# Hybrid decoder step on one Trainium2 core: query norms in compact rows, chunks 3 and 5 of the input projection by seven half-sized products

## The chip, the cores and the metric

The kernel runs on one core of a Trainium2 chip. The metric is the device time of one execution in microseconds (us), start to end, for the prompt (256 tokens) and the sample group (8 tokens) together.

## The reference

One layer of a hybrid decoder over 264 tokens, width 1024. All data are float32.

```python
h = rmsnorm(x, attn_norm_w)
proj = jnp.einsum('btd,de->bte', h, w_in)          # 1024 -> 6400
xin, bg, cg, q, k, v, g_conv, g_attn = jnp.split(proj, ...)
conv_out, conv_state = causal_short_conv(cg * xin, conv_prefix, conv_w)   # width 3
y_conv = bg * conv_out
q = rmsnorm(q.reshape(b, T, N_HEADS, HEAD_DIM), q_norm_w)   # per head, 16 heads of 64
k = rmsnorm(k.reshape(b, T, N_KV, HEAD_DIM), k_norm_w)
y_attn = window attention (window 128, relative bias, sinks)
merged = sigmoid(g_conv) * y_conv + sigmoid(g_attn) * y_attn
x = x + merged @ w_out
x = x + moe_ffn(rmsnorm(x))      # top 4 of 32 experts, clamped SwiGLU
```

Outputs are y for both groups and the new convolution, key and value states.

## The kernel before

**Order of the work.** The kernel first projects the normed tokens, held transposed (features on partitions, 264 tokens as columns), then runs attention and convolution in between, then the output projection and routing, then streams the weights of all 32 experts (two at a time, `pair`). The weights of `w_in` come in 13 chunks of 2 MB (`w_in_chunk`): chunk 0 holds k and v; chunks 1 and 2 q; 3 cg; 4 xin; 5 bg; 6 gc; 7 cg; 8 xin; 9 bg; 10 gc; 11 and 12 ga. cg, xin, bg and gc appear twice, for the two halves of the features. An ordinary chunk is four tiles of 128 features, numbered through by `tile_list` (tiles 2 to 5 are chunk 1, 10 to 13 chunk 3, 14 to 17 chunk 4, 18 to 21 chunk 5), each eight products of 128x128 by 264 columns into one of two banks of `pB`. A query tile holds two heads' halves and takes sixteen 128x64 products that run in pairs.

**Chunks by seven products.** The chunks named in `SEVEN` (line 81: 6, 7, 9 to 12) are computed as a 2x2 block product with seven block products instead of eight (the Strassen-Winograd scheme). One product (`product`, line 2020, slots s = 0 to 6) is eight matmuls of 132 columns. It needs four sums of weight blocks (`add_weights`, L1409, on VectorE, into a ring slot of their own), sums of token blocks shared by all chunks (`side1` to `side4`, L1422), and VectorE reads the results out of PSUM (`seven`, L1345). Products 0 to 3 use the banks of `pB`, 4 to 6 the upper half of `pA`, where attention scores of two key blocks also lie.

**The order is written out by hand** in `plan` (line 196) and the tables above it. `STEPS` is one list of steps, walked by each engine in turn; a step is placed "after" a tile or a slot, and `slot(c, s)` is product s of chunk c. `SUM_STEPS` places the weight sums, `SIDE_STEPS` the token sums, `UNIT_STEPS` the seven steps of each attention unit (scores, bias, peak, exp, norm, turn, values). `FILLS_OF` counts how many fills of the two banks of `pM` (`misc_bank`) each step makes.

**Query norms.** Every query tile is squared on ScalarE (L1074). For two tiles at a time TensorE adds the 64 squares of each head by four 64x64 matmuls of ones ("squares"), so that each sum stands on all 64 rows of its head. VectorE scales them (L1508, L1512), ScalarE takes the root (L1077), VectorE the reciprocal of the whole 128x264 tile (L1518) and the product with the queries (L1520).

**Convolution.** On an xin tile VectorE multiplies it with cg (L1473), then does the three taps: three operations on the 256 prompt columns (L1482, L1485) and three on the 8 sample columns, with the convolution state as input for two of them (L1483, L1487). On tile 0 of them it waits for the stores of keys and values, whose staging rows in `yc` the result overwrites.

**Ring and queues.** The ring has six slots of 2 MB. `RING` lists weights and sums in order; each entry takes the next slot and waits until TensorE has left the chunk six entries earlier. SyncE (SP) issues all weight loads in order, and between them some of the 32x32 block moves of the attention probabilities (`move_blocks`; the rest are on GpSimd's queue). Loads of expert weights start when TensorE starts chunk 12.

## Time and profile before

| what | us |
|---|---|
| median of 3 runs | 1150.89 (1149.01 to 1151.21) |
| profiled execution | 1149.04 |
| its span, first to last instruction | 1147.1 |
| TensorE busy | 1094.3 (95%) |
| VectorE busy | 445.6 (39%) |
| ScalarE busy | 184.8 (16%) |
| GpSimd busy | 88.7 (8%) |

The chain that ended last is 61% TensorE and 37% DMA. Busy shares are averages over stages: the projection, up to about 200 us, and the experts' stream behind it have different limits, so the stages are to be read apart.

### The profile page before, as it was taken

How to read it: one execution, taken by the hardware profiler on the slowest of the kernel's cores; microseconds unless marked ns; L12 is line 12 of the kernel's file. 1: busy time of each engine (PE TensorE's matmuls, PEld its weight loads, DVE VectorE, ACT ScalarE, POOL GpSimd, SP SyncE). 2: the span in 40 equal slices, each digit the busy share in tenths (PEclk: the TensorE clock that was granted, in tenths of full speed). 3: DMA queues.
4: the chain of work that ended last, by engine and by line, in shares of the span. 5: the costliest groups of instructions: out<-in, count | busy, mean ns of one | idle time of the engine just before them, and what ended most of it. 6: DMA issues, size and time to landing. Idle time of an engine off the chain costs nothing.

```text
span 1147.1 us, 14808 instructions
## 1 busy us (share of the span) xinstructions
PE 1094.3 (95%) x5914; PEld 494.8 (43%) x5943; DVE 445.6 (39%) x882; ACT 184.8 (16%) x394; POOL 88.7 (8%) x161
## 2 busy tenths in 40 slices
PE   9999999999999999999899999999999999999997
PEld 6688899553333333333333333333333333333332
DVE  4867786753343233233223232323232323232322
ACT  2133231211321101010101010101010101010101
POOL 1775115000000000000000000000000000000000
PEclk9999999999999999999999999999999999999999
DMA  9945639999999999999999999999999999999996
GB/s 320 329 135 158 196 92 350 414 359 419 397 419 428 416 432 431 431 431 434 430 431 432 434 431 433 430 431 434 430 433 432 433 432 428 433 434 430 425 424 284
DMA packets 53204, 444.35 MB, mean 387 GB/s; under 512 B 13100, under 2 KB 19372, under 8 KB 35740
## 3 DMA queue, kind: packets, MB, share of 16 engines
q1 hardware_dynamic: 46712, 435.83, 91.3%
q0 software_dynamic: 5600, 7.32, 2.4%
q10 hardware_dynamic: 852, 0.64, 0.2%
q8 instruction: 28, 0.46, 0.2%
q14 instruction: 12, 0.10, 0.0%
HBM read 439.78 MB, written 2.37 MB: 385 GB/s over the span
## 4 chain that ended last, share of the span: by engine, by line
PE 61%; DMA 37%; issue 1%; DVE 1%; ACT 0%; SPq 0%; DVEq 0%
PE pA L2001 31%; PE pB L2001 22%; DMA ring<-in_w_up 21%; DMA ring<-in_w_down 10%; PE pM L2001 6%; DMA area<-in_w_up 5%; PE pM L2004 1%; DMA ring<-in_w_in 1%; PE pA L2004 1%; ACT area L1223 0%; DVE x L1848 0%; SPq L775 0%; DVE conv_row L1762 0%; DVE area L1923 0%; DVE x L1928 0%
## 5 line engine op out<-in xcount | busy, mean ns | idle before, releaser
L2001 PE MATMUL pA<-ring,hn 128*64 128x512 f32 x1536 | 352.6, 602 | 23.2 <-DMA ring<-in_w_up 23.2
L2001 PEld LDWEIGHTS pA<-ring,hn 128*64 128x64 f32 x1536 | 105.3, 137 | 219.1 <-issue 185.5
L2001 PE MATMUL pB<-ring,area 128*64 128x512 f32 (+2 forms) x784 | 171.5, 591 | 6.6 <-DMA ring<-in_w_down 5.8
L2001 PE MATMUL pB<-area,ring 128*128 128x132 f32 (+2 forms) x928 | 140.3, 342 | 0.6 <-DMA ring<-in_w_in 0.6
L2001 PE MATMUL pA<-area,hn 128*64 128x512 f32 x512 | 119.3, 610 | 10.4 <-DMA area<-in_w_up 10.4
L2001 PEld LDWEIGHTS pB<-area,ring 128*128 128x128 f32 (+1 forms) x928 | 115.7, 175 | 22.4 <-issue 3.3
L2001 PEld LDWEIGHTS pB<-ring,area 128*64 128x64 f32 (+2 forms) x784 | 58.5, 136 | 101.2 <-issue 87.8
L1848 DVE TENSOR_TENSOR x<-pM,x 128x512 f32<-128x512 f32 x60 | 40.1, 692 | 147.7 <-PE pM L2001 147.7
L1211 ACT ACTIVATE area<-area 128x512 f32<-128x512 f32 x30 | 18.9, 631 | 385.5 <-DVE area L1831 385.5
L1762 DVE COPY conv_row<-pM 128x512 f32<-128x512 f32 x30 | 20.6, 686 | 146.2 <-PE pM L2001 146.2
L2001 PEld LDWEIGHTS pA<-area,hn 128*64 128x64 f32 x512 | 36.1, 139 | 74.6 <-issue 59.7
L2001 PE MATMUL pB<-area 128*64 128x512 f32 (+2 forms) x300 | 66.8, 549 | 1.2 <-DVE area L1292 1.2
L1831 DVE TENSOR_SCALAR area<-pA 128x512 f32<-128x512 f32 x30 | 20.7, 692 | 92.6 <-PE pA L2001 92.6
L1765 DVE TENSOR_TENSOR hn<-pM,fnorm 128x512 f32<-128x512 f32 x30 | 20.7, 692 | 84.9 <-PE pM L2004 84.5
L2001 PE MATMUL pM<-area 128*32 128x256 bf16 (+2 forms) x353 | 49.0, 327 | 2.7 <-issue 2.4
L1873 DVE COPY area<-pB 64x512 f32<-64x512 f32 x15 | 10.4, 694 | 100.0 <-PE pB L2001 100.0
L2001 PEld LDWEIGHTS pM<-area 128*128 128x128 bf16 (+2 forms) x368 | 18.7, 96 | 51.2 <-issue 35.6
L2001 PEld LDWEIGHTS pB<-area 128*64 128x64 f32 (+2 forms) x300 | 20.8, 131 | 35.5 <-issue 31.0
L2001 PE MATMUL pM<-hn,x 128*128 128x512 bf16 x98 | 30.4, 381 | 2.1 <-issue 2.1
L1409 DVE TENSOR_TENSOR ring<-ring 128x1024 f32<-128x1024 f32 x24 | 29.0, 1217 | 0.1
L1223 ACT ACTIVATE area<-pA 128x512 f32<-128x512 f32 x15 | 9.0, 597 | 120.7 <-PE pA L2004 120.7
L2004 PEld LDWEIGHTS pA<-cst,area 128*128 128x128 f32 x120 | 16.8, 210 | 24.3 <-issue 24.3
(351 smaller groups left out, 942.5 us busy)
## 6 DMA issues: line engine op xcount, KB each, us to landing
ring<-in_w_up SPq DMA_DIRECT2D x36, 4096.0 KB, 29.8
ring<-in_w_down SPq DMA_DIRECT2D x18, 4096.0 KB, 29.0
area<-in_w_up SPq DMA_DIRECT2D x12, 4096.0 KB, 30.2
ring<-in_w_up SPq DMA_DIRECT2D x16, 2048.0 KB, 12.8
area<-in_w_down SPq DMA_DIRECT2D x6, 4096.0 KB, 30.0
ring<-in_w_in SPq DMA_DIRECT2D x22, 1024.0 KB, 12.2
ring<-in_w_down SPq DMA_DIRECT2D x16, 1024.0 KB, 10.6
ring<-in_w_up SPq DMA_DIRECT2D x16, 1024.0 KB, 8.4
```

The lines of the kernel that those rows point to most:

```text
L1211: nc.scalar.activation(early_sig if kind == "first" else sig[:, e, :], early_glu if kind == "first" else glu[:, e, :], ACT.Sigmoid, scale= ...
L1223: nc.scalar.activation(turned, pA[:, 1024:1536], ACT.Copy).then_inc(aT_ready, 1)
L1409: V.tensor_tensor(out, x0, x1, op).then_inc(sums_ready, 1)
L1762: return V.tensor_copy(xrow[:, 512 * half:512 * half + 512], b)
L1765: return V.tensor_tensor(xsT[:, 4 * half:4 * half + 4, :], b.rearrange("p (k s) -> p k s", k=4), fw[:, 4 * half:4 * half + 4, :], ALU.mult)
L1831: V.tensor_scalar(gl, u[:, 0, e], LIMIT, None, ALU.min).then_inc(glu_ready, 1)
L1848: V.tensor_tensor(xo, bank(k), xo, ALU.add).then_inc(misc_free, 1)
L1873: V.tensor_copy(y_pair[64:128, 512:1024], pB[64:128, 1, :]).then_inc(y_ready_dve, 1)
L2001: return pe.matmul(out, w, m, start=start, stop=stop, skip_group_check=True)
L2004: return pe.transpose(out, src, ident[0:src.shape[0], 0:src.shape[0]])
```

## The change

**Query norms.** The eight query tiles form two groups of four. "q_sum" adds the squares of four tiles (eight heads) by four matmuls whose weights are a 128x32 cut of the two-block matrix: 16 columns for one head and 16 for the other. The sums of four tiles lie in four bands of 32 rows, so one scaling, one root (ScalarE) and one reciprocal ("q_inverse") serve eight heads. "q_norm" spreads one row per head back over 64 rows, by four matmuls of 32 rows by 64 columns whose weights are one column of the identity, repeated. VectorE multiplies the queries straight from PSUM. There are two q_sum and four q_norm steps where there were four steps "squares".

**Chunks 3 and 5** join `SEVEN`. Since the queries and the old places of the token sums are in use that early, the sums for these two chunks stand in `yc` and `cx` (`early1`, `early2`, `early4`) and ScalarE copies them to the old places later ("side_move").

**Taps.** The first tap of each tile goes to ScalarE ("first_tap", with the wait for the stores of keys and values), the other two come later on VectorE ("taps") and take the sample columns along. The taps on the convolution state are done for four tiles at once ("state_taps").

**Steps** of attention units 0 and 1 and the sample attention are placed anew. With eight chunks in `SEVEN` the ring's entries shift: weights 5 wait for chunk 0, weights 6 for chunk 2, weights 7 for chunk 3, weights 8 for chunk 5 (before: none, 0, 2 and 4). From weights 9 on each waits for the same chunk as before. The diff, cut:

```diff
-SEVEN = (6, 7, 9, 10, 11, 12)
+SEVEN = (3, 5, 6, 7, 9, 10, 11, 12)
+EARLY_SIDES = (3, 5)
...
-UNIT_STEPS = [(11, 12, 12, 13, 13, 18, 19),
-              (18, 18, 19, 19, 20, slot(6, 5), slot(7, 3)),
+UNIT_STEPS = [(slot(3, 2), slot(3, 4), slot(3, 4), slot(3, 6), slot(3, 6), slot(5, 1), slot(5, 3)),
+              (slot(5, 0), slot(5, 1), slot(5, 2), slot(5, 3), slot(5, 5), slot(6, 5), slot(7, 3)),
...
-SIDE_STEPS = [20, 21, slot(6, 2), slot(6, 3), slot(9, 0)]
-SUM_STEPS = {6: (19, 20, slot(6, 0), slot(6, 1)),
+SIDE_STEPS = [5, 6, 7, 8, slot(9, 0)]
+STATE_TAP_STEPS = [6, slot(7, 4)]
+FIRST_TAP_STEPS = [15, 16, 16, 17, 30, 31, 32, 33]
+TAP_STEPS = [16, 17, slot(5, 0), slot(5, 1), 31, 32, 33, slot(9, 0)]
+SIDE_MOVES = [slot(5, 2), slot(5, 4), slot(6, 0)]
+SUM_STEPS = {3: (7, 8, 9, slot(3, 0)),
+             5: (slot(3, 1), slot(3, 2), slot(3, 6), 14),
+             6: (slot(5, 3), slot(5, 5), slot(6, 0), slot(6, 1)),
...
+    for g, at in enumerate(((6, 7, 8, 9), (slot(3, 1), slot(3, 3), slot(3, 5), slot(3, 6)))):
+        for n, what in enumerate((("q_sum", g), ("q_inverse", g), ("q_norm", (g, 0)), ("q_norm", (g, 1)))):
+            after[at[n]].append(what)
...
-    for n, what in ((13, "s_scores"), (14, "s_exp"), (16, "s_norm"), (18, "s_turn"), (20, "s_values")):
+    for n, what in ((14, "s_scores"), (15, "s_exp"), (16, "s_norm"), (slot(5, 1), "s_turn"), (slot(5, 4), "s_values")):
...
+                elif what == "first_tap":
...
+                    nc.scalar.activation(yc[:, a, 0:SEQ], cx[:, a, 0:SEQ], ACT.Copy,
+                                         scale=cols[:, V_CONV + a:V_CONV + a + 1]).then_inc(tap_ready, 1)
...
+                elif what == "q_inverse":
+                    dve.wait_ge(rt_out, a + 2)
+                    V.reciprocal(q_rows[a], q_rows[a]).then_inc(q_inverted, 1)
+                elif what == "q_norm":
+                    g, n = a
+                    for i in range(2):
+                        dst = qT[:, 4 * g + 2 * n + i, :]
+                        V.scalar_tensor_tensor(out=dst, in0=dst, scalar=cols[:, V_QN:V_QN + 1], in1=misc_bank()[:, 0:NT],
+                                               op0=ALU.mult, op1=ALU.mult).then_inc(misc_free, 1)
...
+                elif what == "taps":
...
+                    link(V.scalar_tensor_tensor(out=yc[:, a, 0:SEQ], in0=cx[:, a, 1:1 + SEQ], scalar=w[1],
+                                                in1=yc[:, a, 0:SEQ], op0=ALU.mult, op1=ALU.add))
+                    link(V.scalar_tensor_tensor(out=yc[:, a, :], in0=cx[:, a, 2:], scalar=w[2],
+                                                in1=yc[:, a, :], op0=ALU.mult, op1=ALU.add))
...
+                elif what == "q_sum":
+                    b = misc_bank()
+                    pe.wait_ge(sq_ready, 5 + 4 * a)
+                    for n in range(4):
+                        mm = matmul(b[32 * n:32 * n + 32, 0:NT], cst[:, C_BLK + 48:C_BLK + 80], squares[4 * a + n + 1])
+                    mm.then_inc(misc_full, 1)
+                elif what == "q_norm":
+                    g, n = a
                     b = [misc_bank(), misc_bank()]
+                    pe.wait_ge(q_inverted, g + 1)
+                    for i in range(2):
+                        r = slice(32 * (2 * n + i), 32 * (2 * n + i) + 32)
+                        for h in range(2):
+                            row_of = ident[r, r.start + 16 * h:r.start + 16 * h + 1].to_broadcast([32, HD])
+                            mm = matmul(b[i][HD * h:HD * h + HD, 0:NT], row_of, q_rows[g][r])
+                        mm.then_inc(misc_full, 1)
```

**What the tables move.** TensorE, from chunk 2's last tiles to the end of chunk 3, before (four full tiles; the matmuls into pM from tmp and rt are "squares", those into pA the scores of unit 0):

```order
L2001 MATMUL pB<-area,ring 64x264 x16
L2001 MATMUL pB<-area,ring 128x264 x8
L2001 MATMUL pM<-tmp,cst 64x264
L2001 MATMUL pM<-rt,cst 64x264
L2001 MATMUL pM<-tmp,cst 64x264
L2001 MATMUL pM<-rt,cst 64x264
L2001 MATMUL pB<-area,ring 128x264 x8
L2001 MATMUL pA<-keys,area 128x128 x8
L2001 MATMUL pB<-area,ring 128x264 x16
```

The same place now; pM 32x264 is q_sum, pM 64x264 q_norm:

```order
L2049 MATMUL pM<-area,cst 64x264 x4
L2049 MATMUL pB<-area,ring 128x132 x16
L2049 MATMUL pM<-area,cst 32x264 x4
L2049 MATMUL pB<-area,ring 128x132 x8
L2049 MATMUL pA<-keys,area 128x128 x8
L2049 MATMUL pB<-area,ring 128x132 x8
L2049 MATMUL pA<-area,ring 128x132 x16
L2049 MATMUL pM<-area,cst 64x264 x4
L2049 MATMUL pA<-area,ring 128x132 x8
L2049 MATMUL pM<-area,cst 64x264 x4
```

Four tiles became seven products, with four norm steps on and between them instead of one behind the first tile.

VectorE between slots 3 and 6 of chunk 3 now (L1390 reads products, L1548 is the reciprocal of eight heads, L1607 to L1622 bias and peak of unit 0, L1553 the queries' multiplication); before, the reciprocals stood behind the single tiles and none behind a product:

```order
L1390 TENSOR_TENSOR rt<-tmp,pB 128x264
L1548 RECIPROCAL area<-area 128x264
L1390 TENSOR_TENSOR area<-rt,pA 128x2x132
L1607 SCALAR_TENSOR_TENSOR area<-pA,area 128x4x128 x2
L1615 TENSOR_REDUCE stat<-area 128x8
L1620 TENSOR_TENSOR stat<-stat,sink 128x8
L1621 TENSOR_SCALAR stat<-stat 128x8
L1622 TENSOR_TENSOR stat<-stat,sink 128x8
L1390 TENSOR_TENSOR area<-rt,pA 128x2x132
L1553 SCALAR_TENSOR_TENSOR area<-area,cols,pM 128x264 x2
L1390 TENSOR_TENSOR area<-tmp,pA 128x2x132
```

What moved: the multiplication of q_norm (1,0), the L1553 row here, stands behind bias and peak of unit 0.

VectorE around bias and peak of unit 1, before (L1491 are the bg tiles, L1617 the turned sample probabilities, L1584 the block transpose of unit 0):

```order
L1491 TENSOR_TENSOR area<-pB,area 128x264
L1617 COPY hn<-pM 128x512
L1584 STREAM_TRANSPOSE area<-hn 128x1024
L1559 SCALAR_TENSOR_TENSOR area<-pA,area 128x640 x2
L1491 TENSOR_TENSOR area<-pB,area 128x264
L1409 TENSOR_TENSOR ring<-ring 128x1024
L1567 TENSOR_REDUCE stat<-area 128x8
L1572 TENSOR_TENSOR stat<-stat,sink 128x8
L1573 TENSOR_SCALAR stat<-stat 128x8
L1574 TENSOR_TENSOR stat<-stat,sink 128x8
```

And now (the first row reads slot (5,1), L1574 and L1576 are the taps of tile 3, L1415 multiplies the result of slot (5,2)):

```order
L1390 TENSOR_TENSOR tmp<-tmp,pB 128x264
L1665 COPY hn<-pM 128x512
L1574 SCALAR_TENSOR_TENSOR area<-area,cols 128x256
L1576 SCALAR_TENSOR_TENSOR area<-area,cols 128x264
L1632 STREAM_TRANSPOSE area<-hn 128x1024
L1607 SCALAR_TENSOR_TENSOR area<-pA,area 128x640 x2
L1415 TENSOR_TENSOR area<-pB,area 128x2x132
L1615 TENSOR_REDUCE stat<-area 128x8
L1620 TENSOR_TENSOR stat<-stat,sink 128x8
L1621 TENSOR_SCALAR stat<-stat 128x8
L1622 TENSOR_TENSOR stat<-stat,sink 128x8
```

A weight sum has left the piece and two taps have come in; the piece now lies between slots of chunk 5 instead of full tiles.

## Rows read from the trace of the kernel before

**Rows 1.** Busy us by stage: span, engines, PEclk, DMA share, GB/s.
```profile
0.00:173.00 173.00, 171.14 (x1354) 138.97 (x1355) 127.31 (x263) 52.48 (x171) 72.82 (x130) 1.00 0.66 204
173.00:240.00 67.00, 66.70 (x430) 47.50 (x429) 44.53 (x122) 13.70 (x33) 15.84 (x32) 1.00 0.98 382
...
500.00:1147.00 647.00, 599.23 (x2884) 215.21 (x2901) 183.49 (x313) 75.45 (x124) 0.00 (x0) 0.99 0.99 425
```

**Rows 2.** What TensorE waited for, 0 to 240 us: total, times, longest.
```profile
PE pB L2001 <- DVE area L1292: 1.2, 1, 1.2
PE pB L2001 <- DMA ring<-in_w_in: 0.6, 1, 0.6
PE pM L2001 <- DVE mask L1752: 0.3, 1, 0.3
```

**Rows 3.** The chain of waits, in order of time: start us, us, what.
```profile
29.95 0.60 PE pM L2001 x8
30.56 7.27 PE pB L2001 x64
...
46.31 7.47 PE pB L2001 x48
...
54.39 3.76 PE pB L2001 x16
...
67.15 18.00 PE pB L2001 x80
85.15 0.44 PE pM L2004 x4
...
90.59 1.01 PE pM L2001 x8
...
96.39 10.96 PE pB L2001 x80
...
171.68 7.20 PE pB L2001 x64
```

**Rows 4.** Timeline of VectorE, 34 to 92 us: start us, us, line, operation.
```profile
34.28 0.49 DVE L1520 SCALAR_TENSOR_TENSOR area<-area,cols,tmp 128x264 f32<-128x264 f32 x1
...
61.39 1.28 DVE L1559 SCALAR_TENSOR_TENSOR area<-pA,area 128x512 f32<-128x512 f32 x2
...
64.37 0.17 DVE L1574 TENSOR_TENSOR stat<-stat,sink 128x8 f32<-128x8 f32 x1
...
85.25 0.43 DVE L1491 TENSOR_TENSOR area<-pB,area 128x264 f32<-128x264 f32 x1 [1.35 <-PE pB L2001]
85.62 0.69 DVE L1617 COPY hn<-pM 128x512 f32<-128x512 f32 x1
86.23 1.24 DVE L1584 STREAM_TRANSPOSE area<-hn 128x1024 f32<-128x1024 f32 x1
87.39 1.52 DVE L1559 SCALAR_TENSOR_TENSOR area<-pA,area 128x640 f32<-128x640 f32 x2
...
92.18 1.48 DVE L1567 TENSOR_REDUCE stat<-area 128x8 f32<-128x1280 f32 x1
```

**Rows 5.** Groups of VectorE, 0 to 200 us: count, busy us, mean ns, idle.
```profile
L1409 DVE TENSOR_TENSOR ring<-ring 128x1024 f32<-128x1024 f32 x24 | 29.0, 1217 | 0.1
L1518 DVE RECIPROCAL tmp<-tmp 128x264 f32<-128x264 f32 x6 | 10.8, 1799 | 2.0 <-ACT tmp L1077 2.0
L1485 DVE SCALAR_TENSOR_TENSOR area<-area,cols 128x256 f32<-128x256 f32 x16 | 7.8, 485 | 0.6
```

**Rows 6.** Timeline of ScalarE, first exponential of unit 1.
```profile
94.30 0.43 ACT L1121 ACTIVATE area<-area,stat 128x160 f32<-128x160 f32 x1 [18.17 <-DVE stat L1574]
```

**Rows 7.** Timeline of SyncE's DMA issues: start us, us of issuing, what.
```profile
82.06 0.92 SPq L762 DMA_DIRECT2D ring<-in_w_in  x2
102.20 3.41 SPq L747 DMA_DIRECT2D hn<-area  x5
...
185.74 0.34 SPq L840 DMA_DIRECT2D ring<-in_w_up  x1
```

More of the change, by code:

```diff
@@ L202, in plan @@
     after[0].append(("square_in", 0))
[L203 to L210 removed]
+    after[2] += [("square", 0), ("qknorm", 0), ("bias_table", 0)]
+    for g, at in enumerate(((6, 7, 8, 9), (slot(3, 1), slot(3, 3), slot(3, 5), slot(3, 6)))):
+        for n, what in enumerate((("q_sum", g), ("q_inverse", g), ("q_norm", (g, 0)), ("q_norm", (g, 1)))):
+            after[at[n]].append(what)
+    for j in range(1, 9):
+        after[j + 1].append(("square_in", j))
     after[3].append(("v_rows", 0))
@@ L218, in plan @@
         after[step].append(("sides", n))
+    for n, step in enumerate(SIDE_MOVES):
+        after[step].append(("side_move", n))
+    for t in range(KT):
+        after[FIRST_TAP_STEPS[t]].append(("first_tap", t))
+        after[TAP_STEPS[t]].append(("taps", t))
+    for n, step in enumerate(STATE_TAP_STEPS):
+        after[step].append(("state_taps", n))
     for c in SEVEN:
@@ L261 @@
           ("gather", 1), ("count", 1), ("gather", 2)]
-FILLS_OF = {"slot": 0, "sides": 0, "sums": 0, "half": 0, "tile": 0, "square_in": 0, "split": 0, "qknorm": 0, "scores": 0, "bias": 0, "exp": 0, "norm": 0, "turn": 0, "peak": 0, "s_norm": 0, "s_exp": 0, "out": 0, "rms": 0,
+FILLS_OF = {"slot": 0, "sides": 0, "sums": 0, "half": 0, "tile": 0, "square_in": 0, "side_move": 0, "q_inverse": 0, "first_tap": 0, "taps": 0, "state_taps": 0, "split": 0, "qknorm": 0, "scores": 0, "bias": 0, "exp": 0, "norm": 0, "turn": 0, "peak": 0, "s_norm": 0, "s_exp": 0, "out": 0, "rms": 0,
             "v_rows": 0, "k_rows": 0, "state_cols": 0, "cache_cols": 0, "conv_rows": 0,
-            "s_split": 0, "part": 0, "ahead": 0, "gather": 0, "s_scores": 2, "squares": 2}
+            "s_split": 0, "part": 0, "ahead": 0, "gather": 0, "s_scores": 2, "q_norm": 2}
 FILL, _n = {}, 0
@@ L414, in build @@
         rstd = tmp[:, 1, :]
-        squares = [tmp[:, 0, :], tmp[:, 1, :], rt[:]]
+        squares = [tmp[:, 0, :]] + 2 * [ya[:, 4 + n, :] for n in range(4)]
+        q_rows = [cx[:, 6 + g, 2:] for g in range(2)]
         table = [one.take(8 * w).rearrange("p (h s) -> p h s", h=8) for w in WIDTH]
@@ L670, in build, with in_pairs @@
         side4 = hn[:, 1, 256:256 + K2 * HALF].rearrange("p (k n) -> p k n", k=K2)
+        early1 = yc[:, 4:6, :].rearrange("p k n -> p (k n)").rearrange("p (k n) -> p k n", k=K2)
+        early2 = yc[:, 6:8, :].rearrange("p k n -> p (k n)").rearrange("p (k n) -> p k n", k=K2)
+        early4 = cx[:, 4:6, 2:].rearrange("p a (b n) -> p a b n", b=2)
+        def in_pairs(side):
+            return side.rearrange("p (a b) n -> p a b n", b=2)
         side3 = [one.take(KT * NT // 4).rearrange("p (k n) -> p k n", k=K2), b12]
@@ new lines, in _ @@
+                elif what == "qknorm":
+                    dve.wait_ge(rt_out, 1)
+                    link(V.reciprocal(squares[0], squares[0]))
+                    link(V.scalar_tensor_tensor(out=kT, in0=kT, scalar=cols[:, V_KN:V_KN + 1], in1=squares[0],
+                                                op0=ALU.mult, op1=ALU.mult))
+                    V.tensor_copy(kR[:], kT[:, 0:SEQ][:, ::-1]).then_inc(qk_normed, 1)
+                elif what == "q_sum":
+                    V.tensor_scalar(q_rows[a], misc_bank()[:, 0:NT], 1.0 / HD, EPS, ALU.mult, ALU.add).then_inc(misc_free, 1)
+                elif what == "q_inverse":
[7 more added lines that the diff above has]
+                                               op0=ALU.mult, op1=ALU.mult).then_inc(misc_free, 1)
+                    if a == (1, 1):
+                        dve.wait_ge(misc_free, FILL["q_norm", (1, 1)])
@@ L2063, in product @@
                     for k in range(K2):
-                        mm = matmul(b[:, HALF * n:HALF * n + HALF], w[:, k, 128 * n:128 * n + 128], m[:, k, :],
+                        mm = matmul(b[:, HALF * n:HALF * n + HALF], w[:, k, 128 * n:128 * n + 128],
+                                    m[:, k // 2, k % 2] if s == 6 and early else m[:, k, :],
                                     start=(first and n == k == 0), stop=(k == K2 - 1))
```

127 lines of the change are left out of this document (59 added, 68 removed).

## The prediction

> **What bounds the kernel now.** I read the busy time by stage first [rows 1]. Up to 173 us TensorE is busy for 171.1 of 173 us while the DMA engines are at 0.66 of their time. From 173 us on the DMA share is 0.98 and 0.99. The granted clock is 1.00 up to 240 us, the upper of its two levels (2.4 GHz), and 0.99 in the last stage, so the clock plays no part. The waits of TensorE come next [rows 2]: up to 240 us it waits for anything in three places, 2.1 us in all, and none of them lies in the projection. In order of time its work is an unbroken row of products [rows 3]. So the projection is bound by TensorE with VectorE just behind it. The loads of the expert weights, which set the second half, are issued as TensorE frees the ring (the first at 185.74 us [rows 7], at the start of chunk 12). A microsecond won or lost on TensorE before that moves the whole stream by a microsecond. That is the measure for each part.
>
> **The path's own work.** An ordinary tile costs 18.00 / 5 = 3.60 us and a chunk of four 14.40; a product of the scheme costs 7.20 / 4 = 1.80 us and a chunk of seven 12.60 [rows 3]. Two chunks: **-3.60 us**.
> Query norms: before, four steps of 0.60 us each (one stands at 29.95 [rows 3]). Now six: two that sum four heads' squares into 32 rows each, four that spread them back. None of these shapes is in the trace. A step can't be shorter than one pass of its 264 columns, and a query tile does eight such passes in 7.27 / 2 = 3.64 us, so 0.45; if its four matmuls ran one after another it would be 4 x 0.45 = 1.8. The nearest row is the old step, also four matmuls on parts of the array, at 0.60, and I take that: 6 x 0.60 - 4 x 0.60 = **+1.2 us** (bounds +0.3 and +8.4).
> Interruptions: the pair of tiles that starts after a norm step at 46.31 takes 7.47 instead of 7.24 (3.64 + 3.60), and the tile at 54.39 takes 3.76 instead of 3.60 [rows 3]; query tiles after a norm step show nothing (7.27 at 30.56). Three more places now return to full-width products: **+0.45 us**. The Trainium skill's page TensorEngine Tiling (Array Packing), under Key Properties, says that changing the tiling mode drains TensorE. By that rule every one of the six steps would pay on both sides, where the query tiles above pay nothing; its consequence is weighed as rival C.
> Sum of TensorE's work alone: -3.6 + 1.2 + 0.45 = **-1.95 us**. Everything else is whether VectorE keeps up.
>
> **VectorE's work.** It loses eight single reciprocals for two (six fewer, 1.80 us each [rows 5], 10.8 us), loses the first convolution tap of eight tiles to ScalarE and most of the small state taps. It gains eight weight sums of 1.22 us [rows 5], 9.8 us, and a few reads. In total it is lighter, so the sum of its work isn't the danger; the places are. ScalarE is busy for only 52.48 of the first 173 us [rows 1], so its eight moved taps and three side copies have room. I walk VectorE's queue against TensorE at each wait that TensorE got. A read of a PSUM bank holds VectorE for 0.37 us (85.25 to 85.62 [rows 4]).
> (a) Chunk 3's second product, slot (3,1), needs two sums. From the end of tile 7 VectorE has its copy (0.4), the reciprocal (1.8), the transpose of the cached keys (1.2, like the one at 86.23 [rows 4]), two sides (0.7 each, an estimate from the sum of twice the size), two sums (1.2 each), tile 8's copy (0.4) and two query multiplications (0.9): 8.5 us. TensorE does tiles 8 and 9, two norm steps and slot (3,0): 2 x 3.64 + 1.2 + 1.8 = 10.3 us. No stall, with 1.8 us in hand.
> (b) **Second norm step of the second group, chunk 3.** From the end of slot 3 VectorE does: read 0.45 with the hand-over, the new reciprocal 1.80, read 0.35, bias and peak of unit 0 in 3.15 (61.39 to 64.54 [rows 4]), read 0.35, two multiplications of the queries 0.9 (0.49 each and overlapping a little, 34.28 [rows 4]): 7.0 us. TensorE does slots 4 and 5, a norm step and slot 6: 3 x 1.8 + 0.6 = 6.0, with the return 6.15. It then wants the two misc banks back: **+0.8 us** of stall.
> (c) **Slot (5,4).** It writes where unit 1's scores lie, so it waits for the end of "peak" 1. In the kernel before, bias and peak of unit 1 stood between full tiles with 3.6 us each; now they stand inside chunk 5. From the end of slot (5,1): read, and wait for the turned sample probabilities, 0.54; their copy 0.61; taps of tile 3, two dependent steps of 0.485 [rows 5] with their hand-over, 1.05; block transpose 1.16 (86.23 to 87.39); bias 1.55; gate product 0.35; peak to release 2.12 (92.18 to 94.30 [rows 4, 6]). Sum 7.4 us. TensorE needs 0.44 + 1.80 + 1.80 + 1.01 for the turn, slots 2 and 3 and the values [rows 3], with one return 5.2 us: **+2.2 us** of stall. Bounds: nothing if it overlaps in a way I don't see, 2.5 if hand-overs are slower.
> (d) Chunk 6: "exp" 1 now starts at (5,4) and its "norm" waits for VectorE behind a weight sum, so ScalarE, which needs about 0.33 us for each of the eight scalings (416 ns long, overlapping; an estimate from the row at 94.30 [rows 6]), reaches the copy of slot (6,0) about 0.25 us after slot (6,2) wants it, and the sample values may wait 0.1 for their bank: **+0.3 us**.
> (e) Loads: weights of chunks 5, 6 and 7 are issued later (ring slots are shared with two more sums) but tens of microseconds ahead of use. Chunk 8's weights move from 82.06 us [rows 7] to the start of chunk 6, about 101 (99.99 before: 96.39 + 3.60 [rows 3], and 1 us of this sum), and are wanted two chunks later: 0 unless rival B.
> (f) State taps for four tiles at once, side copies on ScalarE, first tap on ScalarE: hidden in the waits that VectorE and ScalarE have in chunk 4 and later, 0. From chunk 6 on TensorE's order is the old one.
>
> **Sum:** -1.95 + 0.8 + 2.2 + 0.3 = +1.35 us. The profiled execution took 1149.04 us (span 1147.1 and 1.94 around it), the low end of three runs (1149.01 to 1151.21, median 1150.89). Its changed twin would take 1150.4; against the median the forecast is **1152.2 us**, a difference of 0.12%. A measurement of this kernel tells about 0.2% (2.3 us) from none, so this counts as the same.
>
> **Rivals.**
> A. *The stalls don't come* and TensorE's saving is all kept: 1150.89 - 1.95 = 1148.9 us. For it: the kernel before has no stall at all in this stretch, and its chunk 7 runs bias and peak of unit 2 in the same slots without one. Against: in chunk 7 neither taps nor a copy of the sample probabilities stand in VectorE's queue, and twice as many value products in TensorE's. Chance 0.23.
> B. *Chunk 8's load meets the block moves* (slower). The moves of unit 1 are issued from 102.20 us on by the SP queue [rows 7], when no weights were loading; now 2 MB go out just before them on the same queue, and unit 1's "norm" ends 1.5 us later. VectorE's transpose in slot (6,5) then waits and holds the sums for chunk 7 behind it. The last move lands about where VectorE arrives (ten moves of 0.68 us, as the five at 102.20 take 3.41 [rows 7], from 103.9 on, and some 2 us to land: about 112.7; VectorE at 113, five products into chunk 6). It decides as soon as a move lands over 1 us later than now; with 2 to 3 us late TensorE loses about that much at slot (7,1): 1154.6 us. Chance 0.16.
> C. *The small products cost more* (slower): the six norm steps take 0.9 to 1.8 us, +1.8 to +7.2 us, 1154 to 1159 us. For it: no row has 32-row weights spread to 64 columns. Against: rows of 64 x 64 and 64 x 32 parts ran together. By the Trainium skill's rule above, at 0.2 us for each of twelve switches, the largest excess that rows 3 show, the interruptions would be 2.4 instead of 0.45 us: 1154.1 us. Chance 0.09.
> The forecast keeps 0.52.
>
> **How the numbers follow.** Forecast case, about 1.3 us to either side by the spread of the runs and of (b) and (c): same 0.76, slower 0.2, faster 0.04. A: faster 0.5, same 0.5. B and C: slower 0.85. Together faster 0.52 x 0.04 + 0.23 x 0.5 = 0.14, slower 0.52 x 0.2 + 0.25 x 0.85 = 0.31, same 0.55. The range goes from A's value less 0.9 for the runs, 1148.0, to 1156.0, which takes in B and the lower part of C.
>
> **What would show it.** Right: TensorE waits of about 0.8 us before a matmul into pM near 65 us, released by VectorE's query multiplication, and about 2.2 us before one into pA near 92 us, released by VectorE's last step of "peak"; norm steps of 0.6 us; chunk 6 starting at 101 us where it was 100.0; the first expert load near 187 us. Wrong: no wait at 92 us and a first expert load near 184 (A), a VectorE wait for a DMA near 113 us (B), norm steps over 0.7 us (C). The forecast also falls if the second half doesn't carry the shift of the first.

## The result, and the profile after

Before: 1149.49 us median (1147.9 to 1151.41, 22 runs on the same chip). Changed: **1154.43 us** median (1150.95 to 1160.98, 22 runs). The ratio is **1.0049, 95% interval 1.0041 to 1.0057**: 0.5% slower, more than the 0.2% that a measurement of this kernel can tell. The forecast was 1152.2 us, "the same": the time lies in its range, the sign that it called likeliest was not the one that came. The changed kernel's runs are 10.0 us apart, those of before 3.5 us. The profiled execution took 1158.04 us (span 1156.2), the third slowest of its 22 runs; what it shows has to be held against other executions, and is, below.

What TensorE of the changed kernel waited for up to 250 us (total, times, longest), against [rows 2]:

```profile
PE pA L2049 <- DVE tmp L1390: 3.5, 1, 3.5
PE pA L2049 <- DVE stat L1622: 2.4, 1, 2.4
PE pB L2049 <- DVE area L1337: 1.2, 1, 1.2
PE pM L2049 <- DVE area L1553: 0.6, 1, 0.6
```

Three waits are new. Two were forecast, with these releasers: 0.6 us in chunk 3 (forecast 0.8) and 2.4 us before slot (5,4) (forecast 2.2). The third, the largest, is the one that the sum had at nothing.

The chain of waits of the changed kernel (start us, us, what), the new norm steps and the chunks, against [rows 3]:

```profile
37.44 0.58 PE pM L2049 x8
38.02 7.27 PE pB L2049 x64
45.29 0.60 PE pM L2049 x8
45.90 3.71 PE pB L2049 x32
49.61 0.60 PE pM L2049 x8
50.21 3.80 PE pB L2049 x32
54.01 0.59 PE pM L2049 x8
54.59 2.00 PE pB L2049 x16
...
66.53 0.67 PE pM L2049 x8
```

A norm step takes 0.58 to 0.60 us on the chain, also those that no row of before showed (0.67 the one behind the wait). The query tile behind one of them takes 3.71 us for 3.64, the two products behind the next 3.80 for 3.60, and the single product behind the third 2.00 for 1.80. So TensorE's own work is about as summed; e7, below, shows its sum.

TensorE's timeline in the changed kernel (start us, us, engine, line, operation, count, and in brackets the wait ahead of it and its releaser):

```profile
94.91 3.50 PE L2049 MATMUL pA<-area,ring 128*128 128x132 f32 x16 [2.37 <-DVE stat L1622]
98.34 1.25 PE L2049 MATMUL pM<-hn 128*64 128x8 f32 x32
...
103.23 7.75 PE L2049 MATMUL pB<-area,ring 128*128 128x132 f32 x64
...
121.66 1.58 PE L2049 MATMUL pA<-keys,area 64*32 64x160 f32 x64 [3.48 <-DVE tmp L1390]
123.17 7.04 PE L2049 MATMUL pB<-area,ring 128*128 128x132 f32 x48
```

Windows of TensorE in the same execution (span, busy us of PE, PEld, DVE, ACT, POOL, then PEclk, DMA share, GB/s):

```profile
94.90:98.40 3.50, 3.50 (x18) 3.26 (x19) 1.94 (x3) 3.50 (x18) 3.08 (x6) 0.55 0.35 91
...
121.60:125.00 3.40, 3.34 (x72) 2.88 (x73) 3.37 (x6) 0.65 (x2) 0.00 (x0) 0.65 1.05 387
```

Behind each of the two long waits the products ran at the lower of TensorE's two levels (1.2 GHz) for a while: the 16 matmuls of slot (5,4) take 3.50 us where 2.04 is its time at full clock (e7 below), and the next stretch behind the second wait 7.04 where the kernel before takes 5.67:

```profile
115.73 5.67 PE L2001 MATMUL pB<-area,ring 128*128 128x132 f32 x48
```

Chunk 6 starts at 103.23 us and not at 99.99; the first copy of its slot (6,0) comes late from ScalarE, so its first four products take 7.75 where 7.36 is the time of four in a row (+0.4).

Where the third wait comes from stands on the other engines. The queue of SyncE's DMA issues in the changed kernel (start us, us of issuing, what), against [rows 7], and two rows of VectorE's timeline (the first, in chunk 3, is taken up in the last part):

```profile
103.65 2.18 SPq L786 DMA_DIRECT2D ring<-in_w_in  x2
106.87 4.50 SPq L771 DMA_DIRECT2D hn<-area  x5
111.42 4.12 SPq L771 DMA_DIRECT2D conv_row<-area  x5
...
194.56 0.82 SPq L864 DMA_DIRECT2D ring<-in_w_up  x2
```

```profile
57.16 2.48 DVE L1455 TENSOR_TENSOR ring<-ring 128x1024 f32<-128x1024 f32 x2 [2.07 <-DMA ring<-in_w_in]
...
119.62 1.25 DVE L1632 STREAM_TRANSPOSE area<-hn 128x1024 f32<-128x1024 f32 x1 [4.22 <-DMA conv_row<-area]
```

DMA issues of the changed kernel between 95 and 120 us (KB each, median us from issue to landing):

```profile
hn<-area SPq DMA_DIRECT2D x5, 32.0 KB, 6.3
hn<-area POOLq DMA_DIRECT2D x5, 32.0 KB, 5.6
conv_row<-area POOLq DMA_DIRECT2D x5, 32.0 KB, 4.8
conv_row<-area SPq DMA_DIRECT2D x5, 32.0 KB, 4.6
```

The same moves of SyncE in the kernel before, between 98 and 118 us:

```profile
hn<-area SPq DMA_DIRECT2D x5, 32.0 KB, 2.0
conv_row<-area SPq DMA_DIRECT2D x5, 32.0 KB, 2.3
```

Chunk 8's weights (2 MB, the row at 103.65 us) go out just ahead of unit 1's block moves on the same queue. A move (a copy of 32 KB; hn and conv_row are where unit 1's blocks go) then takes 4.50 / 5 = 0.90 us to issue, where it took 3.41 / 5 = 0.68 [rows 7], and lands after 4.6 to 6.3 us instead of 2.0 to 2.3. VectorE waits 4.22 us for the last, everything in its queue behind the transpose is late, and TensorE waits 3.48 us. On POOL's queue, which carries the other half of the moves, they land after 4.8 and 5.6 us instead of 1.9, but take no longer to issue (2.89 us for five, 2.90 before). On this the Trainium skill, page DMA: Bandwidth & Descriptors, section Queues, rings and completion order, says that descriptors are taken in ring order within a queue and that each DMA engine goes round between queues packet by packet; the slower landings on both queues agree with that.

The first expert load goes out at 194.56 us, before at 185.74 [rows 7]: +8.8 us, and the profiled executions differ by 9.0. So the second half carries the shift, as assumed. In parts, of this one execution: -1.95 own work; +0.65, +2.37 and +3.48 waits; +0.4 slot (6,0); +1.6 and +1.6 for the two stretches at a lower clock (3.50 + 1.25 instead of 2.04 + 1.10 in e7; 1.58 + 7.04 instead of 1.32 + 5.67 in the kernel before); +0.4 a later start of the first products. Together 8.55; 0.3 I can't place. The medians differ by 4.9 us only. Without the lower clock (3.2) and the later start (0.4) the parts come to 4.95, but no trace shows that a median execution is one of that kind.

### The profile page after: what moved, and what is told of

It reads as the page before. It is cut to its first block, busy times and chain, and to the rows that moved or that the text cites. A ratio compares the mean times of both kernels' runs of the same rounds, so it can differ in the third digit from the quotient of the medians.

```text
span 1156.2 us, 15036 instructions
## 1 busy us (share of the span) xinstructions
PE 1096.6 (95%) x6026; PEld 500.0 (43%) x6055; DVE 437.8 (38%) x858; ACT 187.9 (16%) x398; POOL 88.3 (8%) x161
## 3 DMA queue, kind: packets, MB, share of 16 engines
HBM read 439.78 MB, written 2.37 MB: 382 GB/s over the span
## 4 chain that ended last, share of the span: by engine, by line
PE 59%; DMA 37%; DVE 2%; issue 1%; SPq 1%; ACT 0%; DVEq 0%
PE pA L2049 31%; DMA ring<-in_w_up 21%; PE pB L2049 20%; DMA ring<-in_w_down 10%; PE pM L2049 6%; DMA area<-in_w_up 5%; PE pM L2052 1%; DMA ring<-in_w_in 1%; SPq L771 1%; PE pA L2052 1%; DMA conv_row<-area 0%; DVE area L1607 0%; DVE stat L1615 0%; ACT area L1268 0%; ACT area L1173 0%
## 5 line engine op out<-in xcount | busy, mean ns | idle before, releaser
L2049 PE MATMUL pB<-area,ring 128*128 128x132 f32 (+2 forms) x928 | 127.7, 329 | 0.5 <-DMA ring<-in_w_in 0.4
L2049 PEld LDWEIGHTS pB<-area,ring 128*128 128x128 f32 (+1 forms) x928 | 108.2, 177 | 18.8 <-issue 2.7
L1455 DVE TENSOR_TENSOR ring<-ring 128x1024 f32<-128x1024 f32 x32 | 38.7, 1217 | 2.2 <-DMA ring<-in_w_in 2.1
L2049 PE MATMUL pA<-area,ring 128*128 128x132 f32 x288 | 36.1, 285 | 2.4 <-DVE stat L1622 2.4
L2049 PEld LDWEIGHTS pA<-area,ring 128*128 128x128 f32 x288 | 34.5, 196 | 4.1 <-issue 3.6
```

The lines of the kernel that those rows point to most:

```text
L1455: V.tensor_tensor(out, x0, x1, op).then_inc(sums_ready, 1)
L2049: return pe.matmul(out, w, m, start=start, stop=stop, skip_group_check=True)
```

## The experiments

Theory 1: the savings on TensorE are real, and are given back by waits of the order in which VectorE's and SyncE's queues are filled. Rivals: only one of the waits counts; small products or something else cost the time; the lower clock is chance. Each kernel was timed in 5 rounds beside the kernel before on its chip (e1, e2, e4, e6: before 1149.84 us; e7, e8, e9, e11: 1150.01; e3, e10: 1149.76; e12, e13: 1149.87), so the ratios are to be compared. Every trace is of one execution: against the kernel before, the shift of the first expert load and the difference of the medians agree within 1.7 us in every kernel below (e1: 4.35 and 2.8; e3: 2.1 and 0.4; e7: -1.75 and -1.7), and differ by 3.9 us in the profiled execution of the change (8.8 and 4.9).

### e1: the block moves ahead of chunk 8's load

```diff
-MOVED_BEFORE = {9: 1, 12: 2, 13: 3}
+MOVED_BEFORE = {8: 1, 12: 2, 13: 3}
```

> The changed kernel with one thing moved: SyncE issues the block moves of unit 1 ahead of chunk 8's weights instead of behind them. Theory 1 (chunk 8's load slows the moves, VectorE's transpose in slot (6,5) waits 4.2 us for them, TensorE 3.5 us at the scores of unit 2, and then runs 1.6 us at the lower clock): that wait goes, and with it the spread of the runs; left are -1.95 us of TensorE's own work, 0.65 and 2.4 us of stalls and 1.5 us of lower clock, so 1152.0 us, 0.2 to 0.3% above the kernel before, runs within 3 us. Theory 2 (the spread comes from chunk 5's weights, for which VectorE waited 2.1 us near 57 us): no change, about 1154.5 us and runs 8 to 10 us apart.

Measured: 1152.59 us (1150.71 to 1155.48), ratio 1.0026 [1.0017, 1.0034], against the change's 1.0049. The wait for L1390 is gone; that before slot (5,4) stays at 2.37. The moves take 0.68 us each to issue again and land after 2.0 and 2.2 us. The runs are 4.8 us apart, where less than 3 was expected. In chunk 3 TensorE waited 1.52 us in this execution, since VectorE waited 3.19 us for chunk 5's weights, and the clock fell there. SyncE's issues in e1, then windows, behind the wait of 1.52 and behind that of 2.37 us:

```profile
107.58 3.42 SPq L771 DMA_DIRECT2D hn<-area  x5
```

```profile
67.00:71.00 4.00, 3.90 (x16) 2.82 (x17) 2.83 (x7) 2.78 (x16) 4.00 (x9) 0.62 0.29 45
...
97.10:100.50 3.40, 3.34 (x50) 3.19 (x51) 2.95 (x6) 3.40 (x18) 2.92 (x5) 1.00 0.34 88
```

### e2: unit 1's peak earlier

```diff
-UNIT_STEPS = [(slot(3, 2), slot(3, 4), slot(3, 4), slot(3, 6), slot(3, 6), slot(5, 1), slot(5, 3)),
-              (slot(5, 0), slot(5, 1), slot(5, 2), slot(5, 3), slot(5, 5), slot(6, 5), slot(7, 3)),
+UNIT_STEPS = [(slot(3, 2), slot(3, 4), slot(3, 4), slot(3, 6), slot(3, 6), slot(5, 3), slot(5, 4)),
+              (slot(5, 0), slot(5, 1), slot(5, 1), slot(5, 3), slot(5, 5), slot(6, 5), slot(7, 3)),
-TAP_STEPS = [16, 17, slot(5, 0), slot(5, 1), 31, 32, 33, slot(9, 0)]
+TAP_STEPS = [16, 17, slot(5, 0), slot(5, 3), 31, 32, 33, slot(9, 0)]
```

> The changed kernel with VectorE's queue in chunk 5 put in another order: peak of unit 1 right behind its bias, the taps of tile 3 and the block transpose of unit 0 behind slot (5,3), the values of unit 0 behind slot (5,4). Theory 1: TensorE's wait of 2.4 us before slot (5,4) and the 1.5 us that the products behind it lose at the lower clock go; the load of chunk 8 and the moves still meet, so the runs still spread: 1150.5 us (1149.5 to 1152), at most 0.2% above before. Rival: the stall was cover for other work that is late anyway (the sample values, slot (6,0)'s copy on ScalarE), and only 1 us comes back: 1153.4 us.

Measured: 1152.21 us (1151.53 to 1154.93), ratio 1.0026 [1.0015, 1.0038]. That lies between the two forecasts (1150.5 and 1153.4) and just outside the range of the first. The wait before slot (5,4) falls from 2.4 to 0.9 us, but unit 0's values now come 0.9 us late, and chunk 3 has 1.2 us of wait. The collision with chunk 8's load costs 1.8 us in this execution instead of 3.5; in the change itself it was 2.4 in another execution (e12), so how much of that the order does isn't shown.

### e3: both

The lines changed are those of e1 and e2 together.

> e1 and e2 together: the block moves ahead of chunk 8's load on the SP queue, and unit 1's peak one product earlier; the order in chunk 3 is that of the change. Theory 1 (the costs stand one behind another and add up): against e2 (1152.21 us) the 1.8 us wait for unit 1's turned blocks goes, what is left are 0.6 to 1.5 us in chunk 3 and the two waits of 0.9 us in chunk 5: 1150.5 us, 1 us above e4 (1149.49 us). Rival (chunk 3's wait costs nothing in the end): e4's 1149.5 us. Rival 2 (e1 and e2 each removed the same time): 1152.2 us, as each alone.

Measured: 1150.2 us (1149.35 to 1152.99), ratio 1.0004 [0.9995, 1.0012]. In medians over before: the change +4.9 us, e1 +2.8, e2 +2.4, both +0.4. The two parts add up (2.2 and 2.6 saved alone, 4.5 together), and the time is near the theory's 1150.5. In a second set of runs the change stood 7.3 us above before (e12), so what each part saves is known to a few us only.

### e4: all three waits

On top of e3, bias and peak of unit 0 one product later and chunk 5's sums later:

```diff
-UNIT_STEPS = [(slot(3, 2), slot(3, 4), slot(3, 4), slot(3, 6), slot(3, 6), slot(5, 3), slot(5, 4)),
+UNIT_STEPS = [(slot(3, 2), slot(3, 5), slot(3, 5), slot(3, 6), slot(3, 6), slot(5, 3), slot(5, 4)),
-             5: (slot(3, 1), slot(3, 2), slot(3, 6), 14),
+             5: (slot(3, 6), 14, 15, 16),
```

> Both edits before, and two more: bias and peak of unit 0 behind slot (3,5), so that the queries' multiplication stands ahead of them, and the first two weight sums of chunk 5 later, so that VectorE doesn't wait for its load near 57 us. Theory 1: no stall is left in the projection, TensorE keeps its own saving of 1.95 us (less 0.3 for the first copy of chunk 6): 1147.8 us, 0.15% below the kernel before. Rival (something beside the stalls, such as an earlier start of the expert stream that gives nothing back, eats the saving): 1149.5 us or more, the same as before.

Measured: 1149.49 us (1148.3 to 1150.85), ratio 0.9997 [0.9989, 1.0006]. 1147.8 was expected; this is the rival's time, but the trace names what is left. Of TensorE's timeline in e4:

```profile
91.10 2.04 PE L2049 MATMUL pA<-area,ring 128*128 128x132 f32 x16 [0.86 <-DVE stat L1622]
...
95.07 1.08 PE L2049 MATMUL pM<-area,keys 128*64 128x256 f32 x8 [0.90 <-issue]
96.09 3.87 PE L2049 MATMUL pA<-area,ring 128*128 128x132 f32 x32
99.80 7.76 PE L2049 MATMUL pB<-area,ring 128*128 128x132 f32 x64
```

0.86 + 0.90 + 0.4 (7.76 for 7.36) = 2.2 us, which is about what the change saves (1.95). The profile gives the 0.90 no releaser; VectorE's turned copy of unit 0 (L1632, 93.73 us, 1.24 long) ends 0.1 us before, and where it stands earlier (e7) the wait is gone. Chunk 3 has no wait, and the runs are 2.6 us apart instead of 10. The first expert load goes out at 185.94 us, at 185.74 before.

### e6: the collision alone, in the kernel before

```diff
-                    sp.wait_ge(ring_free, before(c))
+                    sp.wait_ge(ring_free, 6 if c == 8 else before(c))
```

> The kernel before with one wait changed: chunk 8's weights are issued when chunk 6 starts, as in the changed kernel, and not when chunk 5 starts. Theory 1 (the load alone, next to unit 1's block moves, makes the late transpose): 1.5 to 5 us above the kernel before and a wider spread, with a wait of VectorE for a DMA near 112 us. Rival (only the later norm of unit 1 in the changed kernel does it): no change, 1149.5 us, since here the moves are issued at 102.2 us and have 1.5 us more.

Measured: 1157.01 us (1156.06 to 1158.27), ratio 1.0063 [1.0050, 1.0076]. TensorE's timeline and SyncE's issues in e6:

```profile
119.09 1.97 PE L2001 MATMUL pA<-keys,area 64*32 64x160 f32 x64 [4.27 <-DVE tmp L1345]
```

```profile
100.67 0.92 SPq L762 DMA_DIRECT2D ring<-in_w_in  x2
102.47 5.77 SPq L747 DMA_DIRECT2D hn<-area  x5
108.28 5.46 SPq L747 DMA_DIRECT2D conv_row<-area  x5
```

This is the strongest run: nothing of the change is in it but when one load is issued, and the third wait appears with its releaser, larger still (4.27 us; a move takes 5.77 / 5 = 1.15 us to issue, hn lands after 8.6 us; VectorE waits 5.0 us for the moves). +7.2 us is more than the wait: from 119.00 to 122.40 us, behind it, the granted clock is 0.59, and the two rows there take 1.6 us more than in the kernel before. The first expert load goes out 6.2 us later; the other 1.0 us of the medians has no place in the trace. That the wait is longer than in the change fits the moves' closer place behind the load (1.8 us instead of 3.2).

### e7 and e13: the queue of VectorE mended further

On top of e4:

```diff
-UNIT_STEPS = [(slot(3, 2), slot(3, 5), slot(3, 5), slot(3, 6), slot(3, 6), slot(5, 3), slot(5, 4)),
-              (slot(5, 0), slot(5, 1), slot(5, 1), slot(5, 3), slot(5, 5), slot(6, 5), slot(7, 3)),
+UNIT_STEPS = [(slot(3, 2), slot(3, 5), slot(3, 5), slot(3, 6), slot(3, 6), slot(5, 0), slot(5, 4)),
+              (slot(5, 0), slot(5, 1), slot(5, 1), slot(5, 3), slot(5, 4), slot(6, 5), slot(7, 3)),
-             6: (slot(5, 3), slot(5, 5), slot(6, 0), slot(6, 1)),
+             6: (slot(5, 4), slot(5, 5), slot(6, 0), slot(6, 1)),
-    for n, what in ((14, "s_scores"), (15, "s_exp"), (16, "s_norm"), (slot(5, 1), "s_turn"), (slot(5, 4), "s_values")):
+    for n, what in ((14, "s_scores"), (15, "s_exp"), (16, "s_norm"), (slot(5, 2), "s_turn"), (slot(5, 4), "s_values")):
```

> The kernel of e4 once more in another order in chunk 5: the turned copy of unit 0 (1.24 us on VectorE) goes into the 2.70 us in which VectorE is idle before chunk 5, the sample group's turned copy (0.69 us) leaves the place before unit 1's bias, the sums (6,0) no longer stand before the copies that unit 0's values wait for, and unit 1's exponents are normed one product earlier. Theory 1 (what keeps the seven-product chunks from paying is only the order of VectorE's queue): e4's waits of 0.86 us before slot (5,4) and 0.90 us before unit 0's values shrink to 0.3 us or less in all, and slot (6,0)'s products no longer wait 0.4 us; 1.5 to 2 us less than e4, 1147.8 us, 0.998 of before. Theory 2 (something else eats each saving): those waits shrink but the time stays at e4's 1149.5 us. Theory 3 (the walk of the queue is wrong): a wait of 0.5 us or more stands at another place before chunk 6 and the time is 1149 us or more.

Measured: **1148.31 us** (1146.74 to 1149.26), ratio **0.9984 [0.9975, 0.9993]**, faster than both kernels. Of TensorE's and VectorE's timelines in e7:

```profile
90.61 2.04 PE L2049 MATMUL pA<-area,ring 128*128 128x132 f32 x16 [0.16 <-DVE stat L1622]
92.58 1.10 PE L2049 MATMUL pM<-hn 128*64 128x8 f32 x32
...
98.23 7.36 PE L2049 MATMUL pB<-area,ring 128*128 128x132 f32 x64
```

```profile
83.83 1.25 DVE L1632 STREAM_TRANSPOSE area<-hn 128x1024 f32<-128x1024 f32 x1
...
86.79 1.55 DVE L1607 SCALAR_TENSOR_TENSOR area<-pA,area 128x640 f32<-128x640 f32 x2
```

The transpose that stood ahead of the peak now lies where VectorE had nothing to do. The wait is 0.16 us, slot (6,0)'s copy is in time, and chunk 6 starts at 98.23 us, 1.76 before the 99.99 of the kernel before. With the wait that is 1.92 us of TensorE's own work, against the 1.95 summed; both executions start chunk 1 at 22.61 us.

> The kernel of e7 once more, on the same chip as the changed kernel. Theory (the change pays once its order is mended): 0.998 to 0.999 of before, about 1148.3 us, 6 us below the changed kernel, in runs less than 3 us apart, and no TensorE wait above 0.5 us between 60 and 170 us. Rival (e7's gain was chance): within 0.0005 of before or above.

Measured, on another chip: 1147.96 us (1146.56 to 1149.62, 11 runs), ratio 0.9985 [0.9976, 0.9994]. The gain holds.

### e8: compact norms and later taps alone

```diff
-SEVEN = (3, 5, 6, 7, 9, 10, 11, 12)
-EARLY_SIDES = (3, 5)
+SEVEN = (6, 7, 9, 10, 11, 12)
+EARLY_SIDES = ()
...
+UNIT_STEPS = [(11, 12, 12, 13, 13, 18, 19),
+              (18, 18, 19, 19, 20, slot(6, 5), slot(7, 3)),
...
+    for g, at in enumerate(((6, 7, 8, 9), (10, 11, 12, 13))):
```

and the taps, side moves, sums of chunk 6 and the sample group's steps behind whole tiles in the same way.

> The change without its seven-product chunks: chunks 3 and 5 are made by four whole tiles each as before the change, the compact norms, the later taps, the early sides and their moves are those of the change. Theory 1 (the sum of the prediction): TensorE's own work is larger than before by 6 norm steps against 4 (1.2 us) and the returns to full width (0.45 us), and no wait is added: 1151.5 us, 1.0014 of before. Rival (the small products cost more than 0.60 us a step, or their answers are late): 1153 us or more with a wait named at a norm step. Rival 2 (VectorE's shorter norms free something on the path): 1150 us or less.

Measured: 1151.2 us (1150.46 to 1153.32), ratio 1.0015 [1.0007, 1.0024]: 1.2 us more than before in the medians, the interval reaching from 0.8 to 2.8, where 1.65 were expected. TensorE also waited 0.65 us for unit 0's copy out of PSUM (L1639), and no wait was expected. Its first expert load goes out 2.2 us later, 1.5 of them TensorE's own work. So compact norms and moved taps without the two chunks cost time. What they buy is room on VectorE (six reciprocals fewer) for the sums of two more chunks; that the chunks would not fit without that room is argued and was not run.

### e9 and e11: does a wait lower the clock?

In e1 the wait of 2.37 us left the granted clock at 1.00, so the fall could be chance. e9 (on e1) makes the wait longer; e11 (on e9) fills it with products and changes nothing else.

```diff
-                    link(V.tensor_reduce(stat[:, 16:24], prob[:, :, 0:WIDTH[q]], AX.X, ALU.max))
+                    for _ in range(3 if a == 1 else 1):
+                        link(V.tensor_reduce(stat[:, 16:24], prob[:, :, 0:WIDTH[q]], AX.X, ALU.max))
```

```diff
+                if (c, s) == (5, 3):
+                    for n in range(4):
+                        for k in range(K2):
+                            matmul(b[:, HALF * (n % 2):HALF * (n % 2) + HALF], s2[:, k, 128 * (n % 2):128 * (n % 2) + 128],
+                                   t2[:, k, :], start=(n % 2 == k == 0), stop=(k == K2 - 1))
```

> The kernel of e1 with VectorE's reduce for unit 1's peak done three times over (same result): 2.96 us more before slot (5,4)'s products, whose wait was 2.37 us in e1. Theory clock (a TensorE idle for more than 2 us comes back at a lower granted clock, so that the profile of the changed kernel lost 1.5 us over its products behind such a wait): the wait is 5.3 us, the granted clock of the 3.4 us behind it is below 0.7, and the time is 2.96 + 1.5 = 4.5 us above e1's 1152.6: 1157.1 us. Theory chance (in e1's profile the clock stayed at 1.00 behind 2.37 us, so the drop belongs to single executions and not to the wait): the clock stays at 1.00 and the time is 1155.6 us.

> The kernel of e9 with TensorE kept at work in the same stretch: the 16 products of slot (5,1) are done twice more into their own bank before slot (5,3) (same result; 3.7 us at full clock), inside the 5.3 us in which TensorE would wait for unit 1's peak. The peak comes no later, so the chunk should go on at the same moment. Theory clock: no long idle, no lower clock behind it: about 1.5 us less than e9. Theory chance: the same time as e9 within its interval. In both the wait before slot (5,4) is 1.6 us.

Measured: e9 ratio 1.0074 [1.0061, 1.0087]; its runs are 1156.16 to 1159.42, median 1157.76, one execution of 5019 us left out (with it the median is 1158.5). e11: 1154.37 us (1153.2 to 1155.44), ratio 1.0038 [1.0025, 1.0051]. Filling the idle time won **3.4 us** in the medians. TensorE's timelines and windows, e9 first, then e11:

```profile
97.77 3.86 PE L2050 MATMUL pA<-area,ring 128*128 128x132 f32 x16 [5.41 <-DVE stat L1623]
101.56 1.52 PE L2050 MATMUL pM<-hn 128*64 128x8 f32 x32
```

```profile
97.77:101.60 3.83, 3.83 (x18) 3.59 (x18) 1.93 (x3) 3.83 (x18) 3.42 (x6) 0.50 0.37 101
101.60:103.00 1.40, 1.40 (x33) 1.39 (x32) 0.86 (x2) 0.09 (x1) 1.40 (x4) 0.67 0.74 194
```

```profile
98.08 2.04 PE L2050 MATMUL pA<-area,ring 128*128 128x132 f32 x16 [1.81 <-DVE stat L1623]
100.11 1.11 PE L2050 MATMUL pM<-hn 128*64 128x8 f32 x32
```

```profile
98.08:101.10 3.02, 3.02 (x48) 2.86 (x48) 2.78 (x5) 3.02 (x15) 2.61 (x5) 1.00 0.26 69
```

The products of slot (5,4) start 0.3 us earlier in e9, and chunk 5's last two start 1.9 us later (103.01 and 101.14 us): 1.82 + 0.41 us are lost at a clock of 0.50 and 0.67, nothing at 1.00. The peak is as late in both to 0.3 us, so the loss hangs on TensorE's idleness. Both profiles are single executions, and these differ by 1.8 us; the 3.4 us of the medians are more than that, and e9's profiled run was its fastest. So e9's fall at 5.41 us is shown to come of the idleness; what decides behind 1.5 to 2.4 us, these two can't tell.

### e10: chunk 5's sums later

On e1, only the sums' steps of e4.

```diff
-             5: (slot(3, 1), slot(3, 2), slot(3, 6), 14),
+             5: (slot(3, 6), 14, 15, 16),
```

> The kernel of e1 with one thing more: the four sums of chunk 5's weights are made later (behind slot (3,6) and in chunk 4, as in e4) and not in chunk 3. In e1 VectorE waited 3.19 us at 57.98 us for the load of chunk 5's weights before the first of these sums, and TensorE then waited 1.5 us before the last norm step of chunk 3. Theory 1 (that load, not only the queue's length, makes the wait in chunk 3 and a part of the spread of the runs): VectorE no longer waits for the load, TensorE's wait in chunk 3 is 0.7 us or less, and the time is 0.8 to 1.5 us below e1's 1152.6: 1151.4 us, with runs less far apart than e1's 4.8 us. Rival (the wait in chunk 3 is the queue's own length, and the load is waited for in parallel to something else): the wait stays at 0.6 us or more at the same place and the time stays at 1152.6 us.

Measured: 1152.32 us (1150.21 to 1154.85), ratio 1.0025 [1.0015, 1.0036]; e1 had 1.0026. VectorE no longer waits for the load, and TensorE's wait in chunk 3 is 0.56 us where e1's execution had 1.5, so the load did make that wait longer. In the medians it can't be seen: 0.8 to 1.5 us less than e1 were expected, and 0.3 came, but the two intervals, each some 2 us wide, would hide 0.9 us. The runs are as far apart (4.6 us), so that load isn't the main source of the spread. The clock stayed at 1.00 in this execution (1150.21 us, the fastest of its runs), behind the wait of 2.37 us before slot (5,4) too.

### e12: the changed kernel once more, no edit

> The changed kernel itself once more, with a second profile. Its first profiled execution (1158.04 us) was 3.6 us above the median of its runs and showed two waits (2.37 us for unit 1's peak, 3.48 us behind unit 1's turned blocks), each with a lower granted clock behind it (0.55 and 0.65). e1 and e10 had the first wait with the clock at 1.00. Theory 1 (the waits are fixed by the program, the collision of chunk 8's load with the block moves too, and only the clock differs from one execution to the next): the same two waits within 0.5 us, and near 1154.4 us the granted clock is lower behind at most one of them. Rival (the second wait itself comes and goes between executions): it is below 2 us or absent in an execution near or below the median.

Measured: 1157.16 us (1153.8 to 1159.51, 6 runs), ratio 1.0059 [1.0043, 1.0075]. TensorE's timeline, and a window behind the first wait (behind the second, from 120.20 to 124.00 us, the granted clock is 0.69):

```profile
94.52 3.62 PE L2049 MATMUL pA<-area,ring 128*128 128x132 f32 x16 [2.37 <-DVE stat L1622]
...
120.19 1.32 PE L2049 MATMUL pA<-keys,area 64*32 64x160 f32 x64 [2.42 <-DVE tmp L1390]
121.58 7.34 PE L2049 MATMUL pB<-area,ring 128*128 128x132 f32 x48
```

```profile
94.90:98.40 3.50, 3.50 (x28) 3.38 (x27) 1.77 (x3) 3.50 (x17) 3.46 (x6) 0.59 0.45 118
```

The wait for the peak is the same to 0.01 us, fixed by the order. That behind the moves is 2.42 instead of 3.48 us: it varies from execution to execution. The clock fell behind both. "Behind at most one" was expected near 1154.4 us; this execution took 1157.0, near the median of its own six runs, and so doesn't decide it. The median is 7.3 us above before where it was 4.9; the two intervals of the ratio overlap.

## Why the prediction was right or wrong

The time lies in the stated range, but the forecast of +1.35 us met +4.9, and two of its steps were wrong. That 1152.2 lies only 2.2 us below 1154.43 is in part luck: it was counted from a median of three runs, 1150.89, and 22 runs give 1149.49.

**Right, with its sizes.** The norm steps (0.60 forecast, 0.58 to 0.60). The sum of TensorE's own work, -1.95 us: e7 shows 1.92. (a) no wait at slot (3,1). (b) 0.8 forecast, 0.65 in the trace and 0.6 to 1.7 in the other kernels with that order; it left out VectorE's wait for chunk 5's weights (2.07 us, over at 57.16 us), so "tens of microseconds ahead of use" in (e) is wrong for that load: its first reader is VectorE's sum, in chunk 3. (c) 2.2 forecast, 2.37 measured in all four executions with that order (the change twice, e1, e10): walking the queue of the engine that is waited for, from the end of one product to the release of the next, was exact to 0.2 us. (d) 0.3 forecast, 0.4. And the second half carries the shift of the first.

**Wrong: the step (e), "0 unless rival B".** Rival B was the mechanism that came, at its place and with the releaser named, and its chance was put at 0.16 by the reckoning that "the last move lands about where VectorE arrives". Its terms were mis-sized: the moves start at 106.87 us, not 103.9. Of these 3.0 us chunk 6 itself is 2.2 late (103.23, where 101 was reckoned), 1.6 of it by the products at a lower clock; the rest is unit 1's norm, behind which the moves start 3.64 us into chunk 6, in e1 and e10 too, not 2.9. They need 4.50 and 4.12 us to issue, not 3.41 each; they land after 4.6 to 6.3 us, not "some 2 us". The two last terms come from rows of a queue with no load on it. The last lands at 119.6 us, where 112.7 was reckoned. e6 shows it alone (+7.2 us), e1 takes it away (the medians stand 2.8 us over before instead of 4.9).

**Wrong: "the clock plays no part".** The reading of 1.00 was of a kernel whose longest wait is 1.2 us [rows 2], and the forecast took it to hold for one with waits that the change itself makes. Where the clock fell it cost 1.6 us at each place in the change, 1.7 in e1 and 2.2 in e9. It doesn't fall each time, and that may be a source of the wider spread: the kernels in which TensorE's new waits are below 1 us (e4, e7, e13) have runs 2.5 to 3.1 us apart, the change 10.0 and 5.7 (e12), e1 4.8, e10 4.6. But e6 and e9, with the longest waits, have 2.2 and 3.3 in five runs each, which would fit only if the clock falls there every time. The mean granted clock listed for each run doesn't settle it: in e9 and e12 the slower runs have the lower one (0.997 at 1156.16 us and 0.988 at 1159.42 in e9), in the change hardly (0.987 at 1160.98 us, but 0.996 at 1160.03). The length of the third wait varies too (3.48 and 2.42 us). The link was not tested by itself.

**Rivals.** A (no waits, all of the 1.95 us kept) fell, but is nearly what e7 and e13 reach by another order: 1.7 and 1.9 us below before. C fell: no norm step is over 0.7 us, and what stands behind one is 0 to 0.20 us longer; the sum of TensorE's own work is 0.03 us off. The Trainium skill's rule of a drain at a change of tiling (page TensorEngine Tiling (Array Packing), Key Properties) may stand behind these 0.20 us, but the two query tiles at 38.02 us (7.27) pay nothing for the same kind of change.

What stays open: when exactly a wait makes the clock fall. In e1 it fell behind the wait of 1.52 us and not behind the later one of 2.37; in e10 behind neither; in both profiles of the change behind the 2.37. Open too are the 0.3 us of the sum, what a median execution of the change looks like, and why e12's six runs are slower against before than the first 22.

## What to carry to other kernels

A change that saves time on the busiest engine is worth what the order of its neighbours' queues leaves of it: walk each queue from the event that starts it to the event that releases, put long steps into the holes that the walk shows, and time the reordered kernel before you drop the change (here +0.5% became -0.16%). When a load moves later, price what it now runs beside: the small transfers behind it on its queue, at durations taken under load and not from an idle queue. And count a wait of some microseconds on TensorE as more than its length.
